# A five-layer transformer kernel: high-weight products first in each opening, the splits behind the norms, and a new order of the first transfers

## The reference, cut to what matters

```python
def first_block(x, ln_g, ln_b, ...):
    for i in range(DEPTH):
        ...
        x = _layernorm(DEEPNORM_ALPHA * x + y, ln_g[i], ln_b[i])
    return x

def modulate(x, g, shift, scale):
    return rmsnorm(x, g) * (1 + scale[:, None, :]) + shift[:, None, :]
```

## Time and profile before

| | |
|---|---|
| median of three runs | 1572.99 us (1571.99 to 1573.62) |
| profiled execution | 1573.46 us |
| its span | 1571.6 us |
| TensorE busy | 1509.9 us (96%) |
| VectorE busy | 1072.6 us (68%) |
| ScalarE busy | 813.4 us (52%) |
| GpSimd busy | 82.3 us (5%) |
| mean DMA rate | 179 GB/s |

### The profile page before, as it was taken

One profiled execution on the slowest core, in us unless ns is written; L12 is line 12 of the kernel. 1 busy time (PEld: TensorE's weight loads), 2 busy tenths in 40 slices (PEclk: granted clock), 3 DMA queues, 4 the chain that ended last, 5 costly groups with the idle time before them and its releaser, 6 DMA issues.

```text
span 1571.6 us, 28860 instructions
## 1 busy us (share of the span) xinstructions
PE 1509.9 (96%) x10141; PEld 1312.1 (83%) x10142; DVE 1072.6 (68%) x2139; ACT 813.4 (52%) x1362; POOL 82.3 (5%) x111
## 2 busy tenths in 40 slices
PE   6999999999999989999999999999999999999997
PEld 5877877896778768777899999999998888888886
DVE  3666656656577576457569997676777888865555
ACT  3675465446456645464456666444444444444544
POOL 1000701100110110000000000000000000000000
PEclk9999999999999999999999999999999999999999
DMA  6553654657446547534645555454544555575562
GB/s 242 178 183 121 215 180 157 203 177 235 163 159 221 175 167 261 167 122 148 214 136 174 182 176 197 155 170 163 170 160 167 174 174 173 175 247 196 190 195 97
DMA packets 78500, 281.42 MB, mean 179 GB/s; under 512 B 9408, under 2 KB 11488, under 8 KB 77152
## 3 DMA queue, kind: packets, MB, share of 16 engines
q1 hardware_dynamic: 74176, 261.97, 49.5%
q0 software_dynamic: 4256, 18.56, 3.5%
HBM read 277.31 MB, written 2.14 MB: 178 GB/s over the span
## 4 chain that ended last, share of the span: by engine, by line
PE 81%; DVE 14%; ACT 2%; issue 2%; DMA 0%; POOL 0%; ACTq 0%; DVEq 0%; POOLq 0%
PE banks L710 23%; PE banks L712 22%; PE banks L711 22%; DVE w_lo L1566 4%; PE banks L1146 2%; PE banks L907 2%; PE banks L866 1%; PE banks L827 1%; PE banks L805 1%; PE banks L917 1%; PE banks L916 1%; DVE arena L2072 1%; PE banks L851 1%; ACT w_hi L1225 1%; PE banks L915 1%
## 5 line engine op out<-in xcount | busy, mean ns | idle before, releaser
L1225 ACT ACTIVATE w_hi<-raw 128x1024 fp32r<-128x1024 f32 x456 | 474.2, 1043 | 525.9 <-PE banks L712 503.2
L1566 DVE TENSOR_TENSOR w_lo<-raw,w_hi 128x1024 fp32r<-128x1024 f32 x456 | 546.8, 1204 | 262.7 <-ACT w_hi L1225 259.4
L710 PE MATMUL banks<-w_hi,xT_hi 128*128 128x512 f32 (+2 forms) x1156 | 451.0, 390 | 16.3 <-DVE w_lo L1566 9.8
L711 PE MATMUL banks<-w_lo,xT_hi 128*128 128x512 f32 (+2 forms) x1156 | 443.5, 384 | 0.0
L712 PE MATMUL banks<-w_hi,xT_lo 128*128 128x512 f32 (+2 forms) x1156 | 443.5, 384 | 0.0
L710 PE MATMUL banks<-xT_hi,w_hi 128*128 128x256 f32 x1360 | 388.1, 285 | 3.9 <-issue 2.0
L711 PE MATMUL banks<-xT_lo,w_hi 128*128 128x256 f32 x1360 | 384.6, 283 | 0.0
L712 PE MATMUL banks<-xT_hi,w_lo 128*128 128x256 f32 x1360 | 384.5, 283 | 0.0
L710 PEld LDWEIGHTS banks<-w_hi,xT_hi 128*128 128x128 f32 x1156 | 218.7, 189 | 63.4 <-DVE w_lo L1566 8.0
L710 PEld LDWEIGHTS banks<-xT_hi,w_hi 128*128 128x128 f32 x1360 | 260.6, 192 | 5.9 <-issue 5.2
L711 PEld LDWEIGHTS banks<-xT_lo,w_hi 128*128 128x128 f32 x1360 | 260.8, 192 | 0.2
(11 more groups left out here) (203 smaller groups left out, 1307.2 us busy)
## 6 DMA issues: line engine op xcount, KB each, us to landing
raw<-stream SPq DMA_DIRECT2D x490, 512.0 KB, 3.6
arena<-ln_in POOLq DMA_DIRECT2D x4, 1024.0 KB, 6.1
arena<-x_spill POOLq DMA_DIRECT2D x3, 1024.0 KB, 10.5
arena<-mod_rows POOLq DMA_DIRECT2D x2, 1536.0 KB, 8.4
raw<-stream SPq DMA_DIRECT2D x6, 256.0 KB, 3.8
arena<-g_in POOLq DMA_DIRECT2D x3, 512.0 KB, 11.7
raw<-stream SPq DMA_DIRECT2D x8, 160.0 KB, 2.4
arena<-arena POOLq DMA_DIRECT2D x2, 512.0 KB, 5.1
```

The costliest lines, as they stand in the source:

```text
L710: pe.matmul(out, stationary[0], moving[0], start=first, stop=False, **k)
L711: pe.matmul(out, stationary[0], moving[1], start=False, stop=False, **k)
L1225: act.activation(part(w_hi[:, s]), part(half_raw(s), True), ACT.Copy).then_inc(piece_hi, 1)
L1566: dve.tensor_tensor(part(w_lo[:, s]), part(half_raw(s), True), part(w_hi[:, s].bitcast(F32)), ALU.subtract).then_inc(piece_lo, 1)
```

## The change

It has three parts. In each opening TensorE's products go in another order: for block 0 high by high and low by high, which need only `w_hi`; then the transposes of block 1; then block 0's products with `w_lo`, with block 1's high by high between them; then block 1's other products, with which the pieces are dropped. The waits are for the single part that a product reads (`evac_act` or `evac_dve`, `piece_hi` or `piece_lo`). On VectorE the splits move behind the norms. In the start, SP issues the identity and both x blocks among the first pieces, GpSimd waits for the fourth piece before it loads anything, ScalarE's silu of `c_col` moves to layer 0's query projection with a square-root table load in its place, all four pieces are split ahead of block 1's evacuation, and TensorE gets 9 and 5 matmuls of zeros (bf16, 128x512, into bank 7) around the first transposes.

```diff
         def _(sp):
+            sp.dma_start(kept[:, 0:P], table_in[:, 0:P]).then_inc(ident_loaded, 16)
             sp.dma_start(x_tok[:, 0], x_in[0:P, :]).then_inc(x_loaded[0], 16)
...
                     summed += use == "sum"
+                    if len(freed) == RAW:
+                        sp.dma_start(x_tok[:, 1], x_in[P:2 * P, :]).then_inc(x_loaded[1], 16)
                     if len(freed) == 2 * RAW:
...
-            load(kept[:, :], table_in[:, 0:KEPT_W], kept_loaded)
-            load(x_tok[:, 1], x_in[P:2 * P, :], x_loaded[1])
...
+            pool.wait_ge(piece_landed[2 * RAW - 1], 16)
+            load(kept[:, P:], table_in[:, P:KEPT_W], kept_loaded)
             load(c_col[:, :], c_in, c_loaded)
...
             def project_opening(unit, turned, turn_other):
 
+                def x_ready(b, half, low=False):
+                    u = turned[2 * b + half]
+                    if low:
+                        pe.wait_ge(evac_dve, u.part_count[0]["dve"])
+                    else:
+                        pe.wait_ge(evac_act, u.part_count[0]["act"])
+
+                def opening_products(b, n, x, w, first=False):
+                    for kt in range(PK):
+                        k, slot = PK * n + kt, (piece[0] + n) % RING
+                        pe.matmul(bank_of(unit, b)[:, 0:unit.cols], x[:, k, b * P:(b + 1) * P],
+                                  w[:, slot].rearrange("p (k n) -> p k n", n=COLS)[:, kt, 0:unit.cols],
+                                  start=(first and k == 0), stop=False, skip_group_check=True)
+
+                def high_by_high(b, half):
+                    x_ready(b, half)
+                    for n in range(2 * half, 2 * half + 2):
+                        pe.wait_ge(piece_hi, piece[0] + n + 1)
+                        opening_products(b, n, xT_hi, w_hi, first=True)
+
+                def high_by_low(b, n):
+                    pe.wait_ge(piece_lo, piece[0] + n + 1)
+                    opening_products(b, n, xT_hi, w_lo)
+
                 bank_free(unit)
-                for b in range(B):
-                    for n in range(RING):
-                        if n % 2 == 0:
-                            wait_put(pe, [turned[2 * b + n // 2]])
-                        if b == 0 and n == RING - 1:
-                            turn_other()
-                        w = take_piece(n if b == 0 else 0)
-                        for kt in range(PK):
-                            mm = block_products(unit, b, bank_of(unit, b), w, PK * n + kt, kt)
-                        if b:
-                            drop_piece(mm)
+                for half in range(2):
+                    high_by_high(0, half)
+                    x_ready(0, half, low=True)
+                    for n in range(2 * half, 2 * half + 2):
+                        opening_products(0, n, xT_lo, w_hi)
+                turn_other()
+                for n in range(2):
+                    high_by_low(0, n)
+                for half in range(2):
+                    high_by_high(1, half)
+                for n in range(2, RING):
+                    high_by_low(0, n)
+                for n in range(RING):
+                    if n % 2 == 0:
+                        x_ready(1, n // 2, low=True)
+                    for kt in range(PK):
+                        k, slot = PK * n + kt, piece[0] % RING
+                        for x, w in ((xT_hi, w_lo), (xT_lo, w_hi)):
+                            mm = pe.matmul(bank_of(unit, 1)[:, 0:unit.cols], x[:, k, P:2 * P],
...
+                    drop_piece(mm)
...
+            def keep_busy(n):
+
+                for _ in range(n):
+                    pe.matmul(banks[:, 7], idle_zeros[:, 0:P], idle_zeros, start=True, stop=True)
+
...
                 turn_block(0)
+                keep_busy(5)
                 project_opening(unit, turned, lambda: turn_block(1))
 
-            pe.wait_ge(kept_loaded, 16)
+            pe.wait_ge(idle_cleared, 1)
+            keep_busy(9)
+            pe.wait_ge(ident_loaded, 16)
...
         def _(act):
...
-            act.wait_ge(c_loaded, 16)
-            act.activation(c_col[:, :], c_col[:, :], ACT.Silu).then_inc(c_silu, 1)
             act.wait_ge(eps_ready, 1)
+            root_table()
...
                     for u in L["xT"][0:2]:
                         evacuate_only(u)
-                    split_ahead(-1)
+                    split_ahead(0)
                     for u in L["xT"][2:4]:
                         evacuate_only(u)
-                    split_ahead(0)
...
                     wait_put(act, L["w_in"])
+                    if l == 0:
+                        act.wait_ge(c_loaded, 16)
+                        act.activation(c_col[:, :], c_col[:, :], ACT.Silu).then_inc(c_silu, 1)
...
         def _(dve):
...
                 take_block(l, 0)
                 norm_block(l, 0)
-                pieces_behind(out, 1)
                 take_block(l, 1)
                 if l == DEPTH - 1:
                     dve.wait_ge(x_half, 4 * l + 2)
                     modulate_block(moba["h"], moba["mod"][:, 1], moba["mod"][:, 0], 0)
                     norm_block(l, 1)
-                for u in turned[0:2]:
-                    evacuate_only(u)
-                pieces_behind(out, 3)
-                if l == DEPTH - 1:
+                    for u in turned[0:2]:
+                        evacuate_only(u)
+                    pieces_behind(out, 1)
                     dve.wait_ge(x_half, 4 * l + 4)
...
                 else:
+                    for u in turned[0:2]:
+                        evacuate_only(u)
                     norm_block(l, 1)
                     dve.wait_ge(x_half, 4 * l + 4)
                 dve.sem_inc(ln_used, 1)
-                pieces_behind(out, RING)
+                pieces_behind(out, RING if l < DEPTH - 1 else 3)
                 for u in turned[2:4]:
                     evacuate_only(u)
+                pieces_behind(out, RING)
...
             scaled(0, right)
+            pieces_behind(out, 1)
             rooted(0)
-            pieces_behind(out, 1)
             evacuate_only(out[2])
...
-            pieces_behind(out, 3)
             rooted(1)
             pieces_behind(out, RING)

```

12 lines of the change are left out of this document (8 added, 4 removed).

## The result

The change takes 1560.35 us, the median of four runs (1558.83 to 1565.03), against 1572.49 (1571.19 to 1573.62) of the kernel before: the ratio is 0.993, 95% interval 0.9918 to 0.9943. It is faster, by 12.1 us, where 18 were forecast (1554.9); the time lies in the upper part of the stated range, 1550 to 1561. Two executions of it were profiled: the first is also the longest of the four (1565.03 us), the second came with the experiments (1559.10 us, span 1557.3). Both are read here, because they differ mainly in one thing, the stretches at half clock (and by 0.8 us in when the fourth piece lands at the start).

What follows compares the result with a forecast made beforehand. TensorE, working 96% of the span, was taken as the bound, so only its stops and low clock could give time. Gains of 10.7 + 3.6 + 0.6 + 3.7 = 18.6 us from 1573.46 gave 1554.9 us, range 1550 to 1561.

Steps and rivals of the forecast that it cites:

- The fourth piece's landing: Start: five transfers of 1.25 us behind x block 0 put the fourth piece's landing at 11.6.
- rival 1: Start: the fourth piece lands 13.0 us after its issue, at about 15.6; start ends 4 us later, 1558.9; chance 0.15.
- the 10.7: Start: the next unit was to start at 22.3 instead of 32.98, a gain of 10.7 us.
- one delay of 0.4 us: Layers 1 to 3: late refill costs 0.4 us per layer, leaving 1.2 net each, 3.6 for three.
- The forecast's own rule: Layers 1 to 3: a piece's landing of 5.4 us delays nothing, one of 6.7 us costs 1.0.
- 6.7 is the longest: Argument against rival 4: 6.7 us is the longest landing near an opening.
- The head start of `ln_in`: Layers 1 to 3: GpSimd's load has a head start, so the refill delay was taken nearer the low end.
- Rival 3: Layers 1 to 3: pieces land 7.4 us after issue and each opening gains nothing, 1558.5; chance 0.07.
- The own gain of 0.6: Opening behind layer 3: gain 0.6 us with the low clock kept; 1.4 more if the low stretch were half as long.
- rival 4: Layers 1 to 3 and behind layer 3: refills take 13.0 us, 6.5 us slower, 1580.0; chance 0.03.
- E: Opening of the last block: high by high needs only `xT_hi`; gain 3.7 us, bounds 2 and 4.
- Rival 2: Start and E: a half-clock stretch of 3.2 us falls on products, 1.6 us each, 1558.1; chance 0.15.

Runs made afterwards that it cites:

- e12: The change itself run again, unaltered, for a second trace (the second execution): 1560.89 us, ratio 0.9926.
- e8: The change with SP's 568 KB of tables issued behind the eighth instead of the fourth piece: 1560.27 us, ratio 0.9929.
- e1: The change in the start alone, later openings as in the kernel before, the start's products block by block: 1563.37 us, ratio 0.9945.
- e5: The change with `ln_in` and bands loaded after the next opening's pieces are used, `mla_norm` at its old time, start's products block by block: 1554.27 us.
- e3: The change with `ln_in`, `mla_norm` and the bands loaded only once the next opening's four pieces are used: 1560.11 us, ratio 0.993.
- e10: e5 with, in layers 1 to 3, the first split ahead of block 1's norm: 1554.04 us, ratio 0.9881.
- e6: e5 with 28 matmuls of zeros ahead of the transposes behind layer 3: 1554.8 us, ratio 0.9887.
- e9: e6 with 14 more matmuls of zeros in TensorE's next stop, ahead of the bands' products: 1553.09 us, ratio 0.9878.
- e4: The change without the 14 products of zeros at the start: 1560.5 us, ratio 0.9927.

## Why the prediction was right or wrong

The sum was 18.6 us; the second execution gained 14.3, and its parts account for the 4.3 that are missing: 1.0 at the start, 1.6 in layers 1 to 3, 1.65 behind layer 3. The median is some 1.3 us above that execution.

**Start.** Right in mechanism, the transfers bound it, and short by 1.0. The fourth piece's landing was forecast at 11.6; it came at 12.5, and between 12.3 and 13.3 in the traces of the same queue. From its `w_hi` on the forecast took 22.3 - 12.8 = 9.5 us, and 23.27 - 13.57 = 9.7 were measured. The term mis-sized is the landing, by 0.9 us. The pace of 1.25 us was right for four of the five transfers; but the third piece lands 2.2 us behind x block 1 (at 11.2 and 9.0, e12), and 1.8 to 2.5 us behind it in each of the eleven traces with this queue. Why is open; it is not the tables, for e8 has it too. The doubt about the tables behind that piece (rival 1) is answered by e8: they don't matter. Two things under the 10.7 were not seen. The new order of products was counted on, and e1 has the gain without it. And 1.6 us of it are the half clock at 25.7 in the one execution that the forecast started from: it was set at full clock after, without being named before, so that part came out by luck in the second execution and not in the first.

**Layers 1 to 3, the opening itself.** Right: forecast 1.6 us before the refill, and 1.75, 1.8 and 1.7 where the refill is taken out (e5).

**Layers 1 to 3, the refill: the step that failed.** The text takes one delay of 0.4 us for each of the three layers, from landings of 5.4 us in layer 1 and 6.7 in layer 2. For layers 1 and 2 taken together that was right: the first piece took 5.7 and 6.4 us, and the two openings gain 2.3 us together, where 2.4 were forecast. The lateness of the issue (1.1 us behind `ln_in`) came out to 0.05 us. What failed is layer 3, which was given the same price: there `mla_norm` goes out between `ln_in` and the piece, the piece took 7.6 us, and the opening lost 0.3 us instead of gaining 1.2. That is 1.5 of the 1.6 us missing in the layers. The forecast's own rule (1.0 us lost at 6.7) gives 1.9 lost at 7.6, and some 2.0 were lost, so the mechanism is right and the landing time is what was mis-sized. The trace of before had 6.8 us for its one piece in that place, so "6.7 is the longest" was slightly wrong too. e5 shows the two loads apart: 3.6 to 3.7 us with neither, 5.4 with `mla_norm` alone. The head start of `ln_in`, given as the reason for the low end, did not help: `ln_in` was still under way when the piece was issued at 429.8, and landed at 433.8, the piece at 437.4. Rival 3 (7.4 us and no gain) is what came, in layer 3 alone. The forecast also had no term for the half clock that can follow such a stop, some 1.6 us more in the first execution.

**Behind layer 3.** This is the second failed step. The own gain of 0.6 was right for a long low-clock stretch (e5: 0.5); with a stretch half as long (e3, e10) it was 1.1, not the 1.4 more that the text gives, because TensorE then waits for VectorE inside the opening. The refill was not in the term at all, only in rival 4, although 3 MB of loads start there: a landing of 10.3 us, between the 6.7 of before and the 13.0 of that rival. It took 2.1 us in the second execution, and with its short stretch the sum fell 1.65 us short of the forecast. Rival 4's long landing came in part, in the one place where those loads stand, and not in the layers.

**E.** 3.7 forecast, 3.7 measured. The stop of 2.66 us for `xT_lo` became one of 0.63 ahead of the high by high products, and there is no half clock:

```profile
735.29 1.20 PE L794 MATMUL banks<-w_hi,xT_hi 128*128 128x512 f32 x4 [0.63 <-DVE arena L1688]
```

But e1 shows that a third of it is a stretch at half clock that an execution of the old order may also be without.

**Clock.** Rival 2 placed such stretches at the start and in E for good. At the start the first execution has one (which with the later landing makes 2.4 us) and the second has none; in E no trace of the new order has one. Layer 3's opening, which that rival did not name, has one in three of the five traces with the late refill. The forecast, made against one execution, had no term for their spread, and nine executions of the change lie between 1558.8 and 1565.0.

**Range.** The text says that 1561 takes two of the rivals 1 to 3 together; its own prices give 1561.7 for the cheapest pair. No listed case came whole. The measured 1560.35 is made of parts of them: a landing late by 0.9 us at the start (rival 1 had 4), layer 3 without its gain (rival 3 had all three layers), and the long landing behind layer 3 (rival 4).

## What to carry to other kernels

When a change delays the work that frees input buffers, price the refill place by place, from what else is issued in the same microseconds on any queue: a landing time read in one layer held for the next only where the same loads stood beside it (5.7 and 6.4 us beside `ln_in`, 7.6 with `mla_norm` as well, 10.3 beside 3 MB). Either free one buffer early or hold the large load back until the refills are used; in the layers both gave back nearly the whole loss, and a load held back must not have a smaller, urgent one behind it in its queue. Compare traces by the number of the instruction, opening by opening, before believing a median: here it separated four effects of 1 to 2 us each. And look for stretches at half clock in the trace that a forecast starts from, since they may not come again.

## What had not been expected of the hardware

A stretch at half clock follows most stops of TensorE only in some executions: the stop of 1.70 us in two of thirteen traces (e6, e1), the stop of 1.7 to 3.1 us in layer 3 in three of five, the stop of 2.7 to 2.8 us in E in two of three with the old order, but the stop of 3.8 to 4.5 us behind layer 3 in twelve of twelve. With products of zeros in that last one the stretch there was absent (e6), and with the stop of 1.70 us filled as well the mean clock was 0.998 four times out of four (e9). And the profile's clock column shows 1.00 at the beginning of a trace while matmuls there take twice as long (e4: eight transposes in 1.94 us, against 1.06 behind the idle products).
